# In the sixth step of the attention loop the weight unit is subtracted ahead of the compressed batch's mask

## What is computed

```
x = x + 0.5 * swiglu(rms_norm(x, ffn1_norm), ...)
h = rms_norm(x, mix_norm)
... = split(h @ w_in)                     # 12 column groups, 5852 columns in all
y_a = dsa_mixer(...)                      # top-64 keys by an indexer, 8 heads, one shared key/value
y_b = pool_mixer(...)                     # causal pooling, windows 2, 4, 8, 16
y_c = nsa_mixer(...)                      # 8 heads: compressed blocks (cmp), selected (sel), window (win)
x = x + (g_a * (y_a @ proj_a) + g_b * (y_b @ proj_b) + g_c * (y_c @ proj_c)) @ w_out
x = x + 0.5 * swiglu(rms_norm(x, ffn2_norm), ...)
```

## Time and profile before

| | |
|---|---|
| median of 3 runs | 1189.77 us (1189.6 to 1189.79) |
| the profiled execution | 1189.75 us |
| its span, first to last instruction | 1187.9 us |
| outside of the span | 1.85 us |
| mean granted TensorE clock | 0.998 |
| instructions | 18888 |
| read from HBM | 218.58 MB, 185 GB/s over the span |

### The profile page before, as it was taken

The page is one execution under the profiler, slowest core; times in us unless marked ns, Lnnn a source line. Parts: engine busy times, 40 slices in busy tenths (PEclk is TensorE's granted clock), DMA queues, the critical chain, the costliest instruction groups (busy, mean ns, idle before and its releaser), DMA issues.

```text
span 1187.9 us, 18888 instructions
## 1 busy us (share of the span) xinstructions
PE 1175.4 (99%) x6442; PEld 967.1 (81%) x6442; DVE 976.4 (82%) x2103; ACT 616.1 (52%) x1045; POOL 74.9 (6%) x151
## 2 busy tenths in 40 slices
PE   8999999999999999999999999999999999999997
PEld 7888888887778888888888888888877888888886
DVE  7988886678878698888788898875889696988886
ACT  6544446556654454444464444465566535444443
POOL 5300000421000000000000000024100000000000
PEclk9999999999999999999999999999999999999999
DMA  9655554553445465455565555535543554655553
GB/s 377 231 188 177 200 190 164 186 178 115 144 178 177 177 212 196 176 209 181 208 219 206 201 187 212 182 142 186 173 148 112 196 194 153 231 191 201 209 179 142
DMA packets 37143, 223.53 MB, mean 188 GB/s; under 512 B 6752, under 2 KB 9440, under 8 KB 11232
## 3 DMA queue, kind: packets, MB, share of 16 engines
q1 hardware_dynamic: 35360, 216.36, 51.4%
q10 hardware_dynamic: 1696, 6.43, 1.6%
q0 software_dynamic: 32, 0.00, 0.0%
HBM read 218.58 MB, written 1.05 MB: 185 GB/s over the span
## 4 chain that ended last, share of the span: by engine, by line
PE 86%; DVE 9%; ACT 3%; issue 2%; DMA 0%; DVEq 0%; ACTq 0%
PE G L1430 21%; PE G L1431 21%; PE G L1432 21%; DVE wlo L960 3%; PE TO L1432 3%; PE TO L1431 3%; PE TO L1430 3%; PE SC L1432 3%; PE SC L1431 3%; PE SC L1430 3%; ACT probs L765 2%; DVE sm L1188 1%; DVE probs L1215 1%; PE TO L1446 1%; PE TO L1707 1%
## 5 line engine op out<-in xcount | busy, mean ns | idle before, releaser
L960 DVE TENSOR_TENSOR wlo<-raw,whi 128x1024 fp32r<-128x1024 f32 x395 | 468.2, 1226 | 114.6 <-ACT whi L579 112.4
L579 ACT ACTIVATE whi<-raw 128x1024 fp32r<-128x1024 f32 x395 | 396.2, 1053 | 266.8 <-PE G L1432 149.2
L1430 PE MATMUL G<-whi,xhi 128*128 128x512 f32 x1184 | 464.4, 392 | 1.2 <-DVE wlo L1023 0.7
L1432 PE MATMUL G<-whi,xlo 128*128 128x512 f32 x1184 | 458.2, 387 | 0.0
L1431 PE MATMUL G<-wlo,xhi 128*128 128x512 f32 x1184 | 458.1, 387 | 0.0
L1430 PEld LDWEIGHTS G<-whi,xhi 128*128 128x128 f32 x1184 | 222.9, 188 | 54.4 <-issue 5.4
L1432 PEld LDWEIGHTS G<-whi,xlo 128*128 128x128 f32 x1184 | 222.8, 188 | 45.6
L1431 PEld LDWEIGHTS G<-wlo,xhi 128*128 128x128 f32 x1184 | 223.0, 188 | 43.3
L1054 DVE STREAM_TRANSPOSE shared_q<-shared_q 32x128 f32<-32x128 f32 x640 | 193.7, 303 | 8.3
L651 ACT ACTIVATE shared_q<-G,stat 128x256 f32<-128x256 f32 x88 | 41.8, 476 | 78.1 <-PE G L1432 75.5
L1430 PE MATMUL TO<-whi,ybhi 128*128 128x512 f32 x176 | 69.0, 392 | 0.0
(11 more groups left out here) (204 smaller groups left out, 968.5 us busy)
## 6 DMA issues: line engine op xcount, KB each, us to landing
raw<-stream SPq DMA_DIRECT2D x200, 1024.0 KB, 4.8
gates<-w_in ACTq DMA_DIRECT2D x2, 2048.0 KB, 8.6
z<-z SPq DMA_DIRECT2D x32, 64.0 KB, 4.2
x<-x_in SPq DMA_DIRECT2D x4, 256.0 KB, 5.8
raw<-stream SPq DMA_DIRECT2D x2, 512.0 KB, 5.7
small<-small_in ACTq DMA_DIRECT2D x2, 414.5 KB, 3.1
const<-const_in SPq DMA_DIRECT2D x1, 690.0 KB, 11.9
z<-zkv SPq DMA_DIRECT2D x32, 16.0 KB, 2.0
```

Of the source, the lines that this page charges most:

```text
L579: act.activation(whi[s][:, c], raw[s][:, c], ACT.Copy).then_inc(hi_done, 1)
L960: dve.tensor_tensor(wlo[s][:, c], raw[s][:, c], whi[s][:, c].bitcast(F32), ALU.subtract).then_inc(lo_done, 1)
L1430: pe.matmul(o, ahi, bhi, start=first, stop=False)
L1432: return pe.matmul(o, alo, bhi, start=False, stop=last)
```

## The change

In the VectorE queue of the mixer's loop, at step `k` = 5, the subtraction of unit 18 stood behind `mask_and_max(7)`; it stands ahead of it now, between `weigh(6)` and `mask_and_max(7)`. Nothing is added or taken away, no other step is touched, and no other engine's queue. The loop runs once in each of the two layers.

```diff
                     if k + 1 < NB:
                         weigh(k + 1)
-                    if k in (1, 3):
+                    if k in (1, 3, 5):
                         split(l, at, 2 * c + 1 + tok)
                     if k == 6:
                         topk_round()
                         selection_bias()
                     if k and k + LEAD < NB:
                         mask_and_max(k + LEAD)
                     if k == 1:
                         split(l, at, 15)
-                    if k > 3:
+                    if k == 4 or k > 5:
                         split(l, at, 2 * c + 1 + tok)
```

## The result

The changed kernel takes 1193.82 us (median of 6 runs, 1193.08 to 1195.28), the kernel before 1189.68 in the same set; the ratio is 1.0036, with a 95% interval of 1.0025 to 1.0046. So it is slower, by 4.1 us where 3.8 was forecast. The profiled execution took 1193.08 us, with a span of 1191.3.

The account below looks back on a forecast made before the run. TensorE, busy for 99% of the span, was taken as the bound. Unit 20's delays of 1.92 and 1.90 us swallow step 6's gain and add 3.8 to the profiled 1189.75: 1193.6 us, range 1192.8 to 1195.6.

Parts of the forecast that it names:

- The gain: Step 6, second half of chunk 9: TensorE's stall for unit 18 goes, -0.50 us a layer.
- The delay: VectorE from batch 7's mask, 2.25 us late, through uncovered exponentials and weigh(7) to unit 20, 1.92 late (layer 1: 1.90).
- the slack of 0.33: Batch 9's mask waited for TensorE's scores; this only slack in the chain cuts the delay from 2.25 to 1.92 us.
- After that nothing takes it back: From batch 10's mask to the kernel's end: its wait of 0.42 us shifts whole, and TensorE stays late by 1.92.
- The stall: Step 8, second half of chunk 10: TensorE stands 2.5 us for unit 20, and step 6's gain is lost inside it.
- The sum: Both layers together: 1.92 + 1.90 = 3.8 us slower, giving 1193.6 us; chance 0.68.
- the case's own range: Range of the main forecast alone, for the whole kernel: 1192.8 to 1194.0 us.
- the gain stays: Rival at step 8: the 2.25 us delay is hidden before unit 20 is needed, leaving -0.50 a layer, 1188.8 us; chance 0.06.
- half of it is hidden: Rival around batch 8's exponentials and weigh(8): a wait taken as serial overlaps, 0.92 us a layer, 1191.6 us; chance 0.07.
- The falling clock: Rival at step 8's stall: TensorE's clock drops, 1.8 us each; one layer 1195.4 (0.12), both 1197.2 (0.06); chance 0.18.
- whole range: Range taking in the main forecast and the clock's drop in one layer, 0.80 together: 1192.8 to 1195.6 us.

Follow-up runs that it names:

- topk_ahead: Changed kernel with topk_round and selection_bias moved from behind weigh(7) to ahead of it: 1188.6 us, ratio 0.999 to the kernel before.
- layer0_only: Against the changed kernel, layer 1 put back in the old order, so the change is in layer 0 alone: 1191.76 us, ratio 1.0019.
- second set: The changed kernel run once more, unaltered, for its spread: five executions from 1193.66 to 1195.01 us, ratio 1.0041 to the kernel before.
- step7_alone: Kernel before, with unit 20's split ahead of batch 9's mask at step 7 in place of the turn at step 5: 1192.32 us, ratio 1.0021.

## Why the prediction was right

- **The gain** of 0.50 us at step 6 came (no wait there), and was swallowed at step 8, as the prediction said. `topk_ahead` shows it by itself: 1188.6 against 1189.76, 1.16 us, where the prediction has 1.0 if nothing else moved.
- **The delay**: 2.25 us for the mask (2.25 measured); 2.49 us of idleness ahead of `weigh(7)` (2.50); the slack of 0.33 at batch 9's mask used up (no idle row); batch 9's mask, and with it unit 20, late by 1.92 and 1.90 us (1.93 and 1.90). That the uncovered exponentials are the cause is shown by giving the cover back.
- **After that nothing takes it back**: batch 10's wait of 0.43 and the same loss at the masks of layer 1 show it.
- **The stall** of TensorE: 2.5 forecast, 2.57 measured from ready to start.
- **The sum**: 1193.6 against 1193.82, inside the case's own range, and 3.83 us in the loops of the two traces set side by side, where the sum has 3.8. `layer0_only` gives half of it.
- **The rivals**: "the gain stays" and "half of it is hidden" did not happen; the 1.00 us ahead of `weigh(8)` shifted whole. The falling clock did, more often than its chance of 0.18 said: four of 11 executions of the changed kernel lie in the longer group, and four of ten with one layer changed. Two arguments against it were too weak: that the idleness is shorter than that at the kernel's end, and that TensorE is dense on both sides. Its price of 1.8 us was too high for this stall (1.3 between the means of the groups, 1.55 in the one trace that shows it). The mechanism was right, but that the first median came within 0.2 us is in part luck: only one of its six executions belongs to the longer group. In the second set, with three of five, the median was 1194.87, above the case's own range (1194.0) and inside the whole range (to 1195.6), which has the clock's fall in one layer in it.

## What to carry to other kernels

In a loop written out by hand, an instruction that looks late for one reader may be the work that fills another wait on the same queue. Before moving it ahead, ask what runs in its old place, and follow the delay to the next point where the bound engine has no slack. Here the move paid when independent work took the old place (the order with `topk_round` in the gap gained 1.2 us where the order without it lost 4), or when nothing behind the wait was needed soon (units 20 and 22 moved together).

## What the runs showed of the hardware

A stall of TensorE of 2.4 us lowered its clock in one of three traced executions. In the traced execution with layer 0 changed the granted clock was 1.00 up to the end of the stall, 0.50 from some 1.3 us behind it, and back within the stretch from 338 to 340; this cost 1.55 us. In the two traced executions of the changed kernel the same stall passed in both layers without a fall, at a granted clock of 1.00; the stall of 1.62 us of `step7_alone` did so too, and with 5 us of idleness the clock fell in both layers of the traced execution. Why one execution with the 2.4 us stall falls and another does not stays open.

The Trainium skill's page "TensorE: Matmul & The Clock Gate" (Part 1: The HAM clock gate) has the throttled rate as the default state, which activity releases. The 0.50 behind these stalls agrees with it; the two executions without a fall show that a stall of this length is not always enough.
